# The output norm of an encoder layer: squares summed in the feature layout instead of on turned tokens, the gain applied before the turn, evictions by halves

## Chip, cores, metric

One core of a Trainium2 chip runs the whole program. The metric is device time of one execution in microseconds (us). Engines: TensorE (PE, with weight loads shown as PEld), VectorE (DVE), ScalarE (ACT), GpSimd (POOL), SyncE (SP, which here only issues DMAs).

## The reference, cut to what matters

One layer of a streaming encoder over 512 prompt tokens and 64 sample tokens with 1024 features. The last two steps are the down projection with its residual add, and a final RMSNorm with the gain `g_final`:

```
x = x + (silu(conv(a)) * b) @ w_down
...
def rmsnorm(x, g):
    x32 = x.astype(float32)
    y = x32 * rsqrt(mean(x32 * x32, axis=-1, keepdims=True) + EPS)
    return y * g
y_prompt = rmsnorm(xp, g_final)     # (1, 512, 1024)
y_sample = rmsnorm(xs, g_final)     # (1,  64, 1024)
```

## The kernel before

Every engine has its own instruction list, written out by hand; the lists meet at semaphores that count finished steps (`wait_ge`). The residual stream `x_t` lies in feature layout: 128 features on the partitions, `KT` = 8 feature tiles of `T` = 576 tokens (512 prompt, 64 sample) along the row. The outputs are wanted in token layout.

**The last down projection.** The hidden features are worked off in four chunks (`CHUNKS`). After the last chunk's up projection come 16 slots of down products, named by (e, q): e = 0 to 3 is the pair of output tiles 2e and 2e+1, q the factor of the weight block. A slot is 18 matmuls of 128x288 (`down_product`, L2742). Six slot buffers form a ring: ACT rounds a slot's weights to the high part (`slot_hi`, in its list six slots ahead, after the product that freed the buffer), DVE subtracts to get the low part (`slot_lo`). When a tile's products are done, DVE adds the accumulator to `x_t` (L2216) and counts `down_taken`. Tiles 0 and 1 come out of slots (0,2) and (0,3), and from then on tile 2e out of (e,1) and tile 2e+1 out of (e,3); tile 7 is the last. A product that starts a new accumulation waits until the tile before the last one has been taken.

**The output norm.** When the last tile is added, PE turns the five token tiles (four of 128 rows, one of 64) from `x_t` into the four PSUM tensors, eight 128x128 transposes for each (L2803; `final_bank(t)` is `ps[(t+2)%4]`). For every token tile ACT squares the 128x1024 PSUM tile with a running sum per row (L1555) and takes the root (L1558); DVE takes the reciprocal (L2234) and multiplies PSUM tile, reciprocal and a copy of `g_final` on all partitions into `y_tok` (L2235); SP stores the tile (L850, 512 KB, the last 256 KB). The fifth tile is turned when the first has left PSUM. `g_final` is fetched by POOL during the last chunk, spread over all partitions.

**The start.** POOL fetches rows of small parameters (`rows_in`), PE turns them into columns and DVE copies them into `gains`, one column for each 128 features (`NG` = 36).

Of the kernel before, what the change touches and what calls it, by code (L numbers as in the profile page):

```python
# [20 lines left out]
ACT = mybir.ActivationFunctionType  # L21
# [3 lines left out]
P = 128  # L25
# [16 lines left out]
def build(nc, a, o):  # L42

    TP, D = a["x_prompt"].shape[1:]
    TS = a["x_sample"].shape[1]
    T = TP + TS
    H = T // 2
    KT = D // P
# [18 lines left out]
    CHUNKS = [(0, 4), (4, 6), (10, 6), (16, 6)]  # L67
# [6 lines left out]
    DOWN_PAIRS = KT // 2  # L74
# [12 lines left out]
    for s in range(N_ENTRIES + LAG + 1):  # L87
        j, e = divmod(s, ENTRIES)
# [24 lines left out]
    with ctx:  # L113

        slab_bytes = (nc.sbuf_bytes_remaining - 96) // 32 * 32
        slab_at = (nc.sbuf_base + 31) // 32 * 32
        ctx.enter_context(nc.sbuf_tensor("slab", [P, slab_bytes // 4], F32))
        at = {}
        here = [0]

        def place(name, shape, dtype=F32):
            size = 4
            for s in shape[1:]:
                size *= s
# [13 lines left out]
        ident = place("ident", [P, P])  # L138
        causal = place("causal", [P, P])
        causal_s = place("causal_s", [P, DH])  # L140
        mean_w = place("mean_w", [P, P])
        eps = place("eps", [P, 1])
        one = place("one", [P, 1])
        NG = 4 * KT + GROUPS
        gains = place("gains", [P, NG])
        g_mix, g_xq, g_mkv, g_ffn = (gains[:, KT * k:KT * k + KT] for k in range(4))
        pool_scale = gains[:, 4 * KT:NG]
        conv_par = place("conv_par", [P, 4, NF])
        conv_hist = place("conv_hist", [P, 2, NF])
        b_f = place("b_f", [HEADS, 1])  # L150
# [172 lines left out]

        here[0] = at["b_hi"]
        y_tok = place("y_tok", [P, NT + 1, D])
        y_junk = place("y_junk", [P, D])
        g_final = place("g_final", [P, D])

        ps = [ctx.enter_context(nc.psum_tensor(f"ps{n}", [P, 2, 512], F32)) for n in range(4)]
        ACC, SC, OB = ps[0:2], ps[2], ps[3]  # L330
# [2 lines left out]
        def sem(name):  # L333
            return ctx.enter_context(nc.semaphore(name))
# [69 lines left out]
        y_turned, y_root, y_ready = sem("y_turned"), sem("y_root"), sem("y_ready")  # L404
        g_final_landed = sem("g_final_landed")
# [281 lines left out]
        def sums_of(n):  # L687

            return (sum_c, sum_d) if n == 1 else (sum_a, sum_b)

        def final_bank(t):
            return ps[(t + 2) % 4]

# [72 lines left out]
        def _(sp):  # L766
# [78 lines left out]
                raw_tile(r)  # L845

            for t in range(NT + 1):
                sp.wait_ge(y_ready, t + 1)
                y = o["y_prompt"][0, t * P:t * P + P, :] if t < NT else o["y_sample"][0]
                sp.dma_start(y, y_tok[0:y.shape[0], t, :]).then_inc(y_stored, 16)  # L850
            sp.wait_ge(y_stored, 16 * (NT + 1))
# [7 lines left out]
        def _(pool):  # L859
# [19 lines left out]
            pool.dma_start(rows_in[n:NG, 0, :], a["pool_scale"][0].rearrange("(k p) -> k p", p=P)).then_inc(rows_landed, 16)  # L879
            nc.gpsimd.memset(one[:], 1.0).then_inc(consts_ready, 1)  # L880
            nc.gpsimd.memset(mean_w[:], 1.0 / D).then_inc(consts_ready, 1)
            for x in flat_a + flat_b:
# [174 lines left out]
                    pool.wait_ge(conv_ready, 2 * f + 2)  # L1057
                    nc.gpsimd.tensor_copy(gate[:, GAP:GAP + 2], conv_hist[:, :, f + 1]).then_inc(edges_copied, 1)

            pool.wait_ge(slot_used, len(SLOTS) - 4 * DOWN_PAIRS)  # L1060
            pool.dma_start(g_final[:], a["g_final"].rearrange("(x d) -> x d", x=1).partition_broadcast(P)).then_inc(g_final_landed, 16)
            pool.wait_ge(conv_tok_ready, 1)
            pool.dma_start(o["conv_state_prompt"][0, 0].rearrange("s (f p) -> (s f) p", p=P), conv_tok[0:2 * NF, :]).then_inc(stored, 16)
            pool.dma_start(o["conv_state_sample"][0, 0].rearrange("s (f p) -> (s f) p", p=P), conv_tok[2 * NF:4 * NF, :]).then_inc(stored, 16)
# [3 lines left out]
        def _(act):  # L1068
# [6 lines left out]
            def copy(out, x, scale=1.0):  # L1075
                return nc.scalar.activation(out, x, ACT.Copy, scale=scale)  # L1076
# [447 lines left out]
            for g, (kind, k, e, q, _, _) in enumerate(SLOTS):  # L1524
                f0, nf = CHUNKS[k]
                f = f0 + e
                if kind == "up" and q < 3:
                    snapshot(k, e, g, q)
                slot_high(g + AHEAD)
                if kind == "up":  # L1530
                    if q == 0 and e > 0:
                        silu_of(f - 1)
                    if q == 2 and e > 0:
                        hidden_high(f - 1, e - 1)
                    if q == 5:
# [10 lines left out]
                if kind == "down" and f0 + nf == NF and (e, q) == (2, 0):  # L1546
                    act.wait_ge(y_turned, 1)
                    copy(conv_tok[:], ps[2][0:4 * NF, 0, 0:P]).then_inc(conv_tok_ready, 1)


            nc.scalar.activation(stat[:, 62:63], stat[:, 61:62], ACT.Sqrt)
            for t in range(NT + 1):
                r = P if t < NT else TS
                act.wait_ge(y_turned, t + 2)
                nc.scalar.activation(y_junk[0:r, :].rearrange("p (b c) -> p b c", b=2), final_bank(t)[0:r], ACT.Square,  # L1555
                                     accum_out=stat[0:r, 40 + t:41 + t]).then_inc(y_root, 1)
                act.wait_ge(y_root, 2 * t + 1)
                nc.scalar.activation(stat[0:r, 48 + t:49 + t], stat[0:r, 40 + t:41 + t], ACT.Sqrt, bias=eps[0:r],  # L1558
                                     scale=1.0 / D).then_inc(y_root, 1)


        @block.vector
        def _(dve):
# [3 lines left out]
            def after(ins):  # L1567
                link.inc(ins)
                dve.wait_ge(dve_link, link.now)
# [601 lines left out]
            for g, (kind, k, e, q, _, _) in enumerate(SLOTS):  # L2171
# [34 lines left out]
                    slot_sum(g + AHEAD + 1)  # L2206
                else:
                    slot_sum(g + AHEAD + 1)
                    if (e, q) == (0, 0) and k >= 1:
                        dve.wait_ge(hidden_ready, f0 + nf)  # L2210
                        low_hidden(f0 + nf - 1, nf - 1)
# [15 lines left out]
                        if what == "mixed low":  # L2227
                            mixed_low_of(m)

            dve.wait_ge(g_final_landed, 16)  # L2230
            for t in range(NT + 1):
                r = P if t < NT else TS
                dve.wait_ge(y_root, 2 * t + 2)
                after(nc.vector.reciprocal(stat[0:r, 56 + t:57 + t], stat[0:r, 48 + t:49 + t]))  # L2234
                nc.vector.scalar_tensor_tensor(y_tok[0:r, t, :].rearrange("p (b c) -> p b c", b=2), final_bank(t)[0:r],  # L2235
                                               stat[0:r, 56 + t:57 + t], g_final[0:r, :].rearrange("p (b c) -> p b c", b=2),
                                               mult, mult).then_inc(y_ready, 1)


        @block.tensor  # L2240
        def _(pe):
# [53 lines left out]
            for k in range(KT):  # L2295
                values(k)
                if k == 1:
                    pe.wait_ge(rows_landed, 16 * 4)
                    pe.wait_ge(more_rows_landed, 16 * 4)
                    pe.wait_ge(cols_ready, 1)  # L2300
                    turn(bank[:, 0:NG], rows_in[0:NG, 0, :], ident[0:NG, 0:NG])
                    turn(bank[:, 64:64 + 4 * NF], rows_in[0:4 * NF, 1, :], ident[0:4 * NF, 0:4 * NF])
                    turn(bank[:, 192:192 + 2 * NF], rows_in[0:2 * NF, 2, :], ident[0:2 * NF, 0:2 * NF])
                    for g in range(GROUPS):
                        ins = turn(bank[:, 256 + 16 * g:256 + 16 * g + NHIST], hist_tok[0:NHIST, g * P:g * P + P],
                                   ident[0:NHIST, 0:NHIST])
                    ins.then_inc(cols_turned, 1)
                if k == 2:
                    pe.wait_ge(x_scale, 1)
                    pe.wait_ge(cols_ready, 4)  # L2310
                    scale_turn(0, NT, P)
                if k + 2 < KT:
                    h_turn(k + 2)
                if k == 2:
                    pe.wait_ge(scale_rows, 1)
                    scale_turn(NT, NT + 1, TS)
# [472 lines left out]
                    else:  # L2789
                        down_product(g, k, range(half))  # L2790

            tiles = KT * len(CHUNKS)
            pe.wait_ge(down_taken, tiles - 2)
            pe.wait_ge(conv_tok_ready, 1)
            for t in range(NT + 1):
                r = P if t < NT else TS
                if t == NT:
                    pe.wait_ge(y_ready, 1)
                for k in range(KT):
                    if t == 0 and k == KT - 2:  # L2800

                        pe.wait_ge(down_taken, tiles)
                    ins = turn(final_bank(t)[0:r, k // 4, k % 4 * P:k % 4 * P + P], x_t[:, k, t * P:t * P + r], ident[:])  # L2803
                ins.then_inc(y_turned, 1)


_INS = ['x_prompt', 'x_sample', 'cache_fox_k', 'cache_fox_v', 'cache_fox_logf', 'state_pool', 'state_ffn_conv',
# [34 lines left out]
```

## Time and profile before

| | us |
|---|---|
| median of 3 runs | 863.5 (863.03 to 863.79) |
| profiled execution | 863.93 |
| its span, first to last instruction | 862.1 |
| PE busy in the span | 828.7 (96%) |
| DVE busy | 605.0 (70%) |
| ACT busy | 437.3 (51%) |
| POOL busy | 142.8 (17%) |

Matmuls are pipelined and their recorded durations overlap, so the busy time of PE is an upper view of its load. Idle time of an engine that is not the bottleneck costs nothing; what counts is which wait ends last. The last matmul of the last down product ends at 848.93 in the span, so the output norm and its stores are the remaining 13.2.

### The profile page before, as it was taken

What the parts mean: (1) busy time and instruction counts of PE and PEld (TensorE: products, weight loads), DVE (VectorE), ACT (ScalarE), POOL (GpSimd) and SP (SyncE); (2) the same over time, 40 slices, a digit from 0 to 9 for tenths busy, and PEclk for the clock granted to TensorE, in tenths of its full rate; (3) what the DMA queues carried; (4) which work ended last, traced back from release to release, by engine and by line L of the source; (5) the groups of instructions that cost most, each with busy time, mean ns of one, the idle gap of its engine ahead of it and who ended that gap; (6) DMA issues with size and microseconds to landing.
All of it is one profiled execution on the core that took longest, in us unless ns stands there. A gap on an engine that the chain in (4) does not pass through costs nothing.

```text
span 862.1 us, 15501 instructions
## 1 busy us (share of the span) xinstructions
PE 828.7 (96%) x5939; PEld 795.3 (92%) x5939; DVE 605.0 (70%) x1118; ACT 437.3 (51%) x793; POOL 142.8 (17%) x246
## 2 busy tenths in 40 slices
PE   5999999999999999999999999999999999999996
PEld 4798988988997899989998989999999999999995
DVE  3787766677665566554767898998469984699733
ACT  5677666646435554333334444665236652366523
POOL 5015566463000002000000100110001100011100
PEclk9999999999999999999999999999999999999999
DMA  6166434226327533120321323333233323332303
GB/s 215 49 223 169 135 94 113 81 74 233 95 73 284 204 98 122 51 73 2 97 74 50 97 74 100 97 100 110 86 89 89 90 89 95 90 98 86 115 24 111
DMA packets 105141, 91.57 MB, mean 106 GB/s; under 512 B 3008, under 2 KB 96406, under 8 KB 104819
## 3 DMA queue, kind: packets, MB, share of 16 engines
q1 hardware_dynamic: 99939, 73.51, 28.1%
q0 software_dynamic: 5136, 17.17, 6.6%
q8 instruction: 43, 0.70, 0.3%
q14 instruction: 23, 0.19, 0.1%
HBM read 81.32 MB, written 9.35 MB: 105 GB/s over the span
## 4 chain that ended last, share of the span: by engine, by line
PE 80%; DVE 11%; ACT 4%; issue 2%; DMA 2%; SPq 0%; DVEq 0%; ACTq 0%
PE ps L2731 23%; PE ps L434 19%; PE ps L2742 15%; PE ps L2381 4%; PE ps L2274 3%; PE ps L2561 3%; PE ps L2617 2%; PE ps L2567 1%; PE ps L2646 1%; PE ps L2667 1%; DVE w_lo L460 1%; PE ps L2361 1%; DMA x_tok<-in_x_sample 1%; DMA w_raw<-in_w_mk 1%; ACT w_hi L455 1%
## 5 line engine op out<-in xcount | busy, mean ns | idle before, releaser
L2731 PE MATMUL ps<-up_lo,slot_hi 128*128 128x288 f32 x504 | 149.2, 296 | 0.0
L2731 PE MATMUL ps<-up_hi,slot_lo 128*128 128x288 f32 x504 | 148.6, 295 | 0.0
L2731 PE MATMUL ps<-up_hi,slot_hi 128*128 128x288 f32 x504 | 148.5, 295 | 0.0
L1076 ACT ACTIVATE slot_hi<-raw 128x512 fp32r<-128x512 f32 (+2 forms) x118 | 64.6, 554 | 79.9 <-PE ps L2742 55.6
L2731 PEld LDWEIGHTS ps<-up_hi,slot_lo 128*128 128x128 f32 x504 | 95.1, 189 | 0.0
L2731 PEld LDWEIGHTS ps<-up_hi,slot_hi 128*128 128x128 f32 x504 | 95.0, 188 | 0.0
L2731 PEld LDWEIGHTS ps<-up_lo,slot_hi 128*128 128x128 f32 x504 | 94.8, 188 | 0.0
L464 DVE TENSOR_TENSOR slot_lo<-raw,slot_hi 128x512 fp32r<-128x512 f32 (+2 forms) x118 | 70.2, 598 | 31.5 <-ACT slot_hi L1076 31.0
L2742 PE MATMUL ps<-part_hi,slot_hi 128*128 128x288 f32 x352 | 75.5, 295 | 1.9 <-DVE x_t L2216 1.5
L2742 PE MATMUL ps<-part_lo,slot_hi 128*128 128x288 f32 x352 | 75.1, 295 | 0.0
L2742 PE MATMUL ps<-part_hi,slot_lo 128*128 128x288 f32 x352 | 75.0, 294 | 0.0
L1054 POOL COPY a_last<-gate 128x2 f32<-128x2 f32 x44 | 28.1, 668 | 274.3 <-DVE gate L2198 246.3
L434 PE MATMUL ps<-a_hi,w_hi 128*128 128x288 f32 x320 | 69.7, 300 | 2.9 <-DVE w_lo L460 0.9
L460 DVE TENSOR_TENSOR w_lo<-w_raw,w_hi 128x1024 fp32r<-128x1024 f32 x42 | 51.5, 1227 | 24.4 <-ACT w_hi L455 23.8
L434 PE MATMUL ps<-a_lo,w_hi 128*128 128x288 f32 x320 | 68.4, 296 | 0.0
L434 PE MATMUL ps<-a_hi,w_lo 128*128 128x288 f32 x320 | 68.4, 295 | 0.0
L455 ACT ACTIVATE w_hi<-w_raw 128x1024 fp32r<-128x1024 f32 x49 | 51.6, 1053 | 24.1 <-PE ps L434 15.4
L1076 ACT ACTIVATE slot_hi<-row_sum 128x512 fp32r<-128x512 f32 x72 | 45.4, 631 | 36.2 <-PE ps L2731 17.3
L2742 PEld LDWEIGHTS ps<-part_hi,slot_hi 128*128 128x128 f32 x352 | 56.3, 188 | 2.6 <-DVE x_t L2216 2.0
L2742 PEld LDWEIGHTS ps<-part_hi,slot_lo 128*128 128x128 f32 x352 | 56.5, 188 | 0.0
L2742 PEld LDWEIGHTS ps<-part_lo,slot_hi 128*128 128x128 f32 x352 | 56.4, 188 | 0.0
L434 PEld LDWEIGHTS ps<-a_hi,w_hi 128*128 128x128 f32 x320 | 51.4, 189 | 4.5 <-issue 2.5
(408 smaller groups left out, 2078.5 us busy)
## 6 DMA issues: line engine op xcount, KB each, us to landing
raw<-in_w_up SPq DMA_DIRECT2D x36, 512.0 KB, 4.9
raw<-in_w_down SPq DMA_DIRECT2D x12, 768.0 KB, 4.4
w_raw<-in_w_in SPq DMA_DIRECT2D x15, 512.0 KB, 4.1
w_raw<-in_w_o SPq DMA_DIRECT2D x8, 512.0 KB, 4.0
w_raw<-in_w_mq SPq DMA_DIRECT2D x8, 512.0 KB, 4.1
w_raw<-in_w_mo SPq DMA_DIRECT2D x8, 512.0 KB, 4.0
w_raw<-in_w_up SPq DMA_DIRECT2D x8, 512.0 KB, 3.8
w_raw<-in_w_mk SPq DMA_DIRECT2D x6, 512.0 KB, 3.9
```

The source lines that it names most:

```text
L434: mm = nc.tensor.matmul(acc[:, h, 0:H], w[slot][:, c], x[:, k, h * H:h * H + H], start=(k == first and w is w_hi and x is x_hi), stop=(k = ...
L455: nc.scalar.activation(w_hi[slot][:], w_raw[slot][:], ACT.Copy).then_inc(weight_hi_ready, 1)
L460: nc.vector.tensor_tensor(w_lo[slot][:], w_raw[slot][:], w_hi[slot][:].bitcast(F32), ALU.subtract).then_inc(weight_lo_ready, 1)
L464: return nc.vector.tensor_tensor(out, x, hi, ALU.subtract)
L1054: ins = nc.gpsimd.tensor_copy(a_last[:, 2 * g:2 * g + 2, f], gate[:, c:c + 2])
L1076: return nc.scalar.activation(out, x, ACT.Copy, scale=scale)
L2274: ins = mm(b, flat_a[x][:, k * T + t * P:k * T + t * P + P], w[n % 2][:, c], start=(k == 0 and x == 0 and w is w_hi), stop=(k == KT - 1 an ...
L2381: ins = mm(ACC[0][:, half, 0:H], w[n % 2][:, k * P:k * P + P], x[:, k, half * H:half * H + H], start=(k == 0 and w is w_hi and x is a_hi), ...
L2561: ins = mm(banks[t][:, h], x[:, k, t * P:t * P + P], w_hi[slot][:, h * 512:h * 512 + 512], start=(k == 0 and x is mem_hi), stop=False)
L2617: ins = mm(out, flat_b[x][:, col:col + P], kk[:, int(s == SAMPLE), k, :], start=(f == 0 and x == 0 and kk is mk_hi), stop=(f == 1 and x == 1))
L2731: ins = mm(up_bank(k, e, b), w[g % AHEAD][:, m * P:m * P + P], y[:, m, x], start=(first and m == 0 and w is slot_hi and y is up_hi), stop= ...
L2742: ins = mm(acc[:, h, 0:H], w[g % AHEAD][:, m * P:m * P + P], y[:, 2 * m + l, h * H:h * H + H], start=(l == 0 and m == 0 and w is slot_hi a ...
```

## The change

`g_final` becomes eight more columns of `gains`: one more small fetch by POOL and a wait for five such fetches at the start, and no fetch of the spread copy later. During the last down products, ACT makes of each finished `x_t` tile a square (`y_squared`) and a copy multiplied by its gain column (`y_gained`), DVE sums the squares of tiles 0 to 6 in `y_total`. ACT's preparatory root (which loads its function table) moves to slot (1,0). After the last add, DVE squares tile 7 and ACT makes its gained copy. PE turns tiles 0 to 6 of the first three token tiles, then forms the mean squares as one column for each token tile: for each of the five, two products with one column of `mean_w` (which holds 1/1024), one of `y_total` and one of tile 7's squares. Then it turns tile 7 of these three, and the two other token tiles when PSUM is free. ACT takes two roots (four columns, and one for the sample), DVE one reciprocal for all. Each token tile leaves PSUM in halves: ACT multiplies features 0 to 511 by the reciprocal, DVE features 512 to 1023. SP waits for both halves.

```diff
-        NG = 4 * KT + GROUPS
+        NG = 5 * KT + GROUPS
-        pool_scale = gains[:, 4 * KT:NG]
+        pool_scale, g_final = gains[:, 4 * KT:4 * KT + GROUPS], gains[:, 4 * KT + GROUPS:NG]
...
-        y_junk = place("y_junk", [P, D])
-        g_final = place("g_final", [P, D])
+        here[0] = at["up_lo"]
+        y_gained = place("y_gained", [P, KT, T])
+        y_squares = place("y_squares", [P, 2, T])
+        y_total = place("y_total", [P, T])
...
+        def mean_column(t):
+            return ps[1][:, 0, t:t + 1]
+        def y_squared(m):
+            return y_total[:] if m == 0 else y_squares[:, m % 2, :]
+        def y_half(t, h):
+            return y_tok[0:token_rows(t), t, h * 4 * P:(h + 1) * 4 * P]
+        SQUARES_AT = {(1, 0): (0, 1), (1, 2): (2,), (2, 0): (3,), (2, 2): (4,), (3, 0): (5,), (3, 2): (6,)}
+        SUMS_AT = {(1, 1): 1, (1, 3): 2, (2, 1): 3, (2, 3): 4, (3, 1): 5, (3, 3): 6}
...  SP
-                sp.wait_ge(y_ready, t + 1)
+                sp.wait_ge(y_by_act, KT + 2 + t + 1)
+                sp.wait_ge(y_by_dve, 2 + t + 1)
...  POOL
+            pool.dma_start(rows_in[n + GROUPS:NG, 0, :], a["g_final"].rearrange("(k p) -> k p", p=P)).then_inc(rows_landed, 16)
...
-            pool.wait_ge(slot_used, len(SLOTS) - 4 * DOWN_PAIRS)
-            pool.dma_start(g_final[:], a["g_final"].rearrange("(x d) -> x d", x=1).partition_broadcast(P)).then_inc(g_final_landed, 16)
...  ACT, in the loop over slots, after slot_high(g + AHEAD)
+                if kind == "down" and f0 + nf == NF:
+                    if (e, q) == (1, 0):
+                        nc.scalar.activation(stat[:, 62:63], stat[:, 61:62], ACT.Sqrt)
+                    for m in SQUARES_AT.get((e, q), ()):
+                        act.wait_ge(down_taken, LAST_DOWN + m + 1)
+                        if m >= 3:
+                            act.wait_ge(sum_ready, SUMS + m - 2)
+                        nc.scalar.activation(y_squared(m), x_t[:, m, :], ACT.Square).then_inc(x_squared, 1)
+                        copy(y_gained[:, m, :], x_t[:, m, :], g_final[:, m:m + 1]).then_inc(y_by_act, 1)
...  ACT, after the loop
-            for t in range(NT + 1):    # 5 x: Square with row sum from PSUM, then Sqrt
...
+            act.wait_ge(down_taken, LAST_DOWN + KT)
+            copy(y_gained[:, KT - 1, :], x_t[:, KT - 1, :], g_final[:, KT - 1:KT]).then_inc(y_by_act, 1)
+            act.wait_ge(y_turned, 2)
+            nc.scalar.activation(stat[:, 48:48 + NT], ps[1][:, 0, 0:NT], ACT.Sqrt, bias=eps[:]).then_inc(y_by_act, 1)
+            nc.scalar.activation(stat[0:TS, 48 + NT:49 + NT], mean_column(NT)[0:TS], ACT.Sqrt,
+                                 bias=eps[0:TS]).then_inc(y_by_act, 1)
+            act.wait_ge(y_by_dve, 2)
             for t in range(NT + 1):
+                act.wait_ge(y_turned, t + 3)
+                copy(y_half(t, 0), final_bank(t)[0:r, 0], stat[0:r, 56 + t:57 + t]).then_inc(y_by_act, 1)
...  DVE, in the loop, after slot_low and before the tile's add
+                    if f0 + nf == NF and (e, q) in SUMS_AT:
+                        m = SUMS_AT[e, q]
+                        dve.wait_ge(x_squared, X_SQUARED + m + 1)
+                        if m > 1:
+                            dve.wait_ge(sum_ready, SUMS + m - 1)
+                        nc.vector.tensor_tensor(y_total[:], y_total[:], y_squared(m), add).then_inc(sum_ready, 1)
...  DVE, after the loop
-            for t in range(NT + 1):    # 5 x: reciprocal, then PSUM * reciprocal * g_final over 1024
...
+            nc.vector.tensor_tensor(y_squared(KT - 1), x_t[:, KT - 1, :], x_t[:, KT - 1, :], mult).then_inc(y_by_dve, 1)
+            dve.wait_ge(y_by_act, KT + 2)
+            nc.vector.reciprocal(stat[:, 56:57 + NT], stat[:, 48:49 + NT]).then_inc(y_by_dve, 1)
+            dve.wait_ge(y_by_dve, 2)
             for t in range(NT + 1):
+                dve.wait_ge(y_turned, t + 3)
+                nc.vector.tensor_scalar(y_half(t, 1), final_bank(t)[0:r, 1], stat[0:r, 56 + t:57 + t], None,
+                                        mult).then_inc(y_by_dve, 1)
...  PE, after the last down product
-            for t in range(NT + 1):    # 5 x 8 transposes of x_t; tile 4 after tile 0 has left PSUM
...
+            pe.wait_ge(y_by_act, KT - 1)
+            pe.wait_ge(conv_tok_ready, 1)
+            for t in range(3):
+                turn_gained(t, range(KT - 1))
+            pe.wait_ge(sum_ready, SUMS + KT - 2)
+            pe.wait_ge(y_by_dve, 1)
+            for t in range(NT + 1):
+                r = token_rows(t)
+                mm(mean_column(t)[0:r], y_total[:, t * P:t * P + r], mean_w[:, 0:1], start=True, stop=False)
+                ins = mm(mean_column(t)[0:r], y_squared(KT - 1)[:, t * P:t * P + r], mean_w[:, 0:1], start=False, stop=True)
+            ins.then_inc(y_turned, 1)
+            pe.wait_ge(y_by_act, KT)
+            for t in range(3):
+                turn_gained(t, (KT - 1,)).then_inc(y_turned, 1)
+            pe.wait_ge(y_by_act, KT + 2)
+            turn_gained(3, range(KT)).then_inc(y_turned, 1)
+            pe.wait_ge(y_by_act, KT + 3)
+            pe.wait_ge(y_by_dve, 3)
+            turn_gained(NT, range(KT)).then_inc(y_turned, 1)
```

## Rows read from the trace of the kernel before

**Rows 1.** Chain that ended last, from 848: start us, us, what.

```profile
848.96 0.77 DVE x_t L2216
...
849.77 0.45 PE ps L2803 x2
...
850.24 1.12 ACT y_junk L1555 x2
...
851.98 1.28 DVE y_tok L2235
...
857.53 1.28 DVE y_tok L2235
```

**Rows 2.** Timeline of SP's DMA issues at the end: start us, us, what.

```profile
853.29 4.50 SPq L850 DMA_DIRECT2D out_y_prompt<-y_tok  x4
858.83 0.52 SPq L850 DMA_DIRECT2D out_y_sample<-y_tok  x1
```

**Rows 3.** Engine load by stretch; the last columns are TensorE clock, DMA share, GB/s.

```profile
854.00:854.50 0.50, 0.38 (x4) 0.12 (x2) 0.50 (x1) 0.47 (x3) 0.00 (x0) 1.00 0.75 303
...
857.00:857.50 0.50, 0.00 (x0) 0.00 (x0) 0.49 (x2) 0.00 (x0) 0.00 (x0) 1.00 1.02 418
...
861.00:861.50 0.50, 0.00 (x0) 0.00 (x0) 0.00 (x0) 0.00 (x0) 0.00 (x0) 0.50 0.17 41
...
854.00:859.50 5.50, 0.38 (x4) 0.12 (x2) 4.70 (x7) 2.90 (x8) 0.00 (x0) 0.86 0.93 375
859.50:861.20 1.70, 0.00 (x0) 0.00 (x0) 0.00 (x0) 0.00 (x0) 0.00 (x0) 0.50 0.75 174
```

**Rows 4.** Timeline of PE after the last down product.

```profile
848.76 0.82 PE L2803 MATMUL ps<-ident,x_t 128*128 128x128 f32 x6
...
849.77 3.06 PE L2803 MATMUL ps<-ident,x_t 128*128 128x128 f32 x26 [0.19 <-DVE x_t L2216]
```

**Rows 5.** Timelines of weight loads elsewhere: whose matmuls are short, and of the older norms.

```profile
22.95 0.32 PEld L2305 LDWEIGHTS ps<-ident,hist_tok 15*128 15x128 f32 x4
...
275.07 0.90 PEld L2530 LDWEIGHTS ps<-square_sum,mean_w 128*128 128x128 f32 x4
...
398.56 0.19 PEld L2658 LDWEIGHTS ps<-spt,mv_lo 128*128 128x128 f32 x1
398.66 0.19 PEld L2659 LDWEIGHTS ps<-spt,mv_lo 128*128 128x128 f32 x1
```

**Rows 6.** Groups by line and shape: count, busy us, mean ns, idle before.

```profile
L1076 ACT ACTIVATE v_out<-ps,stat 128x512 f32<-128x512 f32 x4 | 2.8, 702 | 0.0
...
L1076 ACT ACTIVATE b_hi<-ps,gains 128x576 fp32r<-128x576 f32 x4 | 3.0, 739 | 0.2 <-PE ps L2474 0.2
...
L1558 ACT ACTIVATE stat<-stat,eps 128x1 f32<-128x1 f32 x4 | 1.2, 294 | 0.1
...
L1904 DVE TENSOR_TENSOR square_sum<-square_sum,squares 128x576 f32<-128x576 f32 x16 | 12.0, 752 | 0.0
...
L1620 DVE COPY inv_rms<-ps 128x512 f32<-128x512 f32 x1 | 0.7, 692 | 0.8 <-PE ps L2257 0.8
...
L1616 DVE RECIPROCAL stat<-stat 128x5 f32<-128x5 f32 x1 | 0.2, 193 | 0.0
```

**Rows 7.** Timeline of ACT and DVE in the last down products.

```profile
822.74 0.53 ACT L1076 ACTIVATE slot_hi<-raw 128x384 fp32r<-128x384 f32 x1 [1.97 <-PE ps L2742]
...
829.87 0.76 DVE L2216 TENSOR_TENSOR x_t<-x_t,ps 128x576 f32<-128x576 f32 x1 [1.20 <-PE ps L2742]
...
835.20 1.28 ACT L1551 ACT_TABLE_LOAD   x1
```

**Rows 8.** Timeline of the start: POOL and PEld; last row: a DMA issue, KB, us to landing.

```profile
8.96 0.94 POOL L867 DMA_DIRECT2D wf_raw<-in_w_in  x1 [2.59 <-DMA x_tok<-in_x_prompt]
...
22.36 0.13 PEld L2301 LDWEIGHTS ps<-ident,rows_in 36*128 36x128 f32 x1 [0.35 <-issue]
...
rows_in<-in_g_mkv POOLq DMA_DIRECT2D x1, 4.0 KB, 5.2
```

More of the change, by code:

```diff
@@ L325, in build @@
         y_tok = place("y_tok", [P, NT + 1, D])
-        y_junk = place("y_junk", [P, D])
-        g_final = place("g_final", [P, D])
+        assert here[0] <= at["whole"]
+        here[0] = at["up_lo"]
+        y_gained = place("y_gained", [P, KT, T])
+        y_squares = place("y_squares", [P, 2, T])
+        y_total = place("y_total", [P, T])
+        assert here[0] <= slab_bytes
         ps = [ctx.enter_context(nc.psum_tensor(f"ps{n}", [P, 2, 512], F32)) for n in range(4)]
@@ L403, in build @@
         conv_tok_ready = sem("conv_tok_ready")
-        y_turned, y_root, y_ready = sem("y_turned"), sem("y_root"), sem("y_ready")
-        g_final_landed = sem("g_final_landed")
+        y_turned, y_by_act, y_by_dve = sem("y_turned"), sem("y_by_act"), sem("y_by_dve")
         stored, y_stored, v_stored = sem("stored"), sem("y_stored"), sem("v_stored")
@@ L692, in final_bank, with token_rows @@
             return ps[(t + 2) % 4]
+        def mean_column(t):
+            return ps[1][:, 0, t:t + 1]
+        def token_rows(t):
+            return P if t < NT else TS
+        def y_squared(m):
+            return y_total[:] if m == 0 else y_squares[:, m % 2, :]
+        def y_half(t, h):
+            return y_tok[0:token_rows(t), t, h * 4 * P:(h + 1) * 4 * P]
+        LAST_DOWN = KT * (len(CHUNKS) - 1)
+        X_SQUARED, SUMS = NT + 1, 2 * (KT + 1)
+        SQUARES_AT = {(1, 0): (0, 1), (1, 2): (2,), (2, 0): (3,), (2, 2): (4,), (3, 0): (5,), (3, 2): (6,)}
+        SUMS_AT = {(1, 1): 1, (1, 3): 2, (2, 1): 3, (2, 3): 4, (3, 1): 5, (3, 3): 6}
         H00, H10, H11, T1, T2, T3, T4 = range(FACTORS)
@@ L878, in _ @@
                 n += KT
[L879 removed]
+            pool.dma_start(rows_in[n:n + GROUPS, 0, :], a["pool_scale"][0].rearrange("(k p) -> k p", p=P)).then_inc(rows_landed, 16)
+            pool.dma_start(rows_in[n + GROUPS:NG, 0, :], a["g_final"].rearrange("(k p) -> k p", p=P)).then_inc(rows_landed, 16)
             nc.gpsimd.memset(one[:], 1.0).then_inc(consts_ready, 1)
@@ L1545, in _ @@
                         whole_high(m)
[L1546 to L1551, printed above, removed]
-            for t in range(NT + 1):
[L1553 to L1559, printed above, removed]
+                if kind == "down" and f0 + nf == NF:
[7 more added lines that the diff above has]
+                        copy(y_gained[:, m, :], x_t[:, m, :], g_final[:, m:m + 1]).then_inc(y_by_act, 1)
+                    if (e, q) == (2, 0):
+                        act.wait_ge(y_turned, 1)
+                        copy(conv_tok[:], ps[2][0:4 * NF, 0, 0:P]).then_inc(conv_tok_ready, 1)
@@ L2228, in _ @@
                             mixed_low_of(m)
-            dve.wait_ge(g_final_landed, 16)
-            for t in range(NT + 1):
[L2232 to L2237, printed above, removed]
+            dve.wait_ge(down_taken, LAST_DOWN + KT)
+            dve.wait_ge(sum_ready, SUMS + KT - 3)
+            nc.vector.tensor_tensor(y_squared(KT - 1), x_t[:, KT - 1, :], x_t[:, KT - 1, :], mult).then_inc(y_by_dve, 1)
+            dve.wait_ge(y_by_act, KT + 2)
+            nc.vector.reciprocal(stat[:, 56:57 + NT], stat[:, 48:49 + NT]).then_inc(y_by_dve, 1)
+            dve.wait_ge(y_by_dve, 2)
+            for t in range(NT + 1):
+                r = token_rows(t)
+                dve.wait_ge(y_turned, t + 3)
+                nc.vector.tensor_scalar(y_half(t, 1), final_bank(t)[0:r, 1], stat[0:r, 56 + t:57 + t], None,
+                                        mult).then_inc(y_by_dve, 1)
         @block.tensor
@@ L2297, in _ @@
                 if k == 1:
-                    pe.wait_ge(rows_landed, 16 * 4)
+                    pe.wait_ge(rows_landed, 16 * 5)
                     pe.wait_ge(more_rows_landed, 16 * 4)
@@ L2790, in _, with turn_gained @@
                         down_product(g, k, range(half))
-            tiles = KT * len(CHUNKS)
-            pe.wait_ge(down_taken, tiles - 2)
+            def turn_gained(t, tiles):
+                r = token_rows(t)
+                for m in tiles:
+                    ins = turn(final_bank(t)[0:r, m // 4, m % 4 * P:m % 4 * P + P], y_gained[:, m, t * P:t * P + r], ident[:])
+                return ins
+            pe.wait_ge(y_by_act, KT - 1)
             pe.wait_ge(conv_tok_ready, 1)
+            for t in range(3):
+                turn_gained(t, range(KT - 1))
+            pe.wait_ge(sum_ready, SUMS + KT - 2)
+            pe.wait_ge(y_by_dve, 1)
             for t in range(NT + 1):
[L2796 to L2804, printed above, removed]
+                r = token_rows(t)
+                mm(mean_column(t)[0:r], y_total[:, t * P:t * P + r], mean_w[:, 0:1], start=True, stop=False)
[9 more added lines that the diff above has]
+            turn_gained(NT, range(KT)).then_inc(y_turned, 1)
 _INS = ['x_prompt', 'x_sample', 'cache_fox_k', 'cache_fox_v', 'cache_fox_logf', 'state_pool', 'state_ffn_conv',
```

## The prediction

> **What bounds the kernel now.** I read the page first: PE is busy 96% of the span, so up to the last down product only work on PE's path counts, and the change adds nothing there. What it rewrites is the end, so I read the chain of waits from 848 on [rows 1]. It leaves PE with the last add of DVE (848.96), passes two transposes, ACT's square over a whole token tile (850.24) and then stays on DVE: five multiplications of 1.28 us, from 851.98 to 858.81, each 1.39 after the one before. By that view DVE's evictions set the end, and halving them should pay. The issues of the stores follow them closely: the first at 853.29, the last at 858.83 [rows 2].
>
> The load by stretch tells what the chain can't [rows 3]. The DMA engines start moving shortly after 854.0 (0.75 of the first half microsecond), and from then to 859.5 they are busy 0.93 of the time at 375 GB/s, with 418 in a half microsecond where the share is 1.02. So the four prompt stores keep the DMA engines nearly full already: 5.50 x 0.93 = 5.12 us of full-share work, which for 4 x 512 KB = 2.10 MB is 410 GB/s. The sample's store has half the bytes but costs 1.70 x 0.75 = 1.28 us, at 174 GB/s; it reads 64 partitions where the others read 128. Together 6.40 us of stream that no eviction can shorten. It takes 7.1 now, from about 854.05 to about 861.15 (0.17 of the last half microsecond that moves anything [rows 3]); only 0.7 of that is gaps. The time from the first store's issue to the end is therefore nearly fixed, and the question is when the first tile is ready, not when the last is.
>
> **The change part by part.** Times below are on the clock of this span; 862.1 of span stand in a profiled execution of 863.93, which lies 0.4 above the median of 863.5. I add the difference to the median.
>
> *Start.* The fifth small fetch costs POOL one more issue. POOL then sits idle for 2.59 us until a prompt tile lands [rows 8], which hides it; without that cover it would be about 0.5. Such fetches land 5.2 us after their issue, and PE first wants them at 22.36 [rows 8], long after. Eight more columns to turn and copy: under 0.05. The removed spread copy of the gain was a 512 KB fetch that nobody on the path waited for. Zero for all this.
>
> *During the last down products.* ACT gains eight operations of 128x576 up to slot (2,2) and six later, at most 0.74 each [rows 6], DVE six sums of 0.75. ACT's slots are 2.4 apart with 0.53 of work [rows 7], so in steady state there is room. The tight place is slot (1,0): after 822.74 + 0.53 the table load of 1.28 (now at 835.20, in idle time [rows 7]), a short root, then square, gain, square: 823.3 + 1.3 + 0.2 + 3 x 0.74 = 827.0. DVE waits for that second square ahead of taking tile 2, so tile 2 is taken not at 825.9 but at 827.0 + 2 x 0.75 = 828.5. Behind it on DVE wait a low part for a slot that PE reaches only about five slots (12 us) later, and PE's start of tile 4, which comes when slot (1,3) ends, just ahead of DVE's add at 829.87 [rows 7]. So 1.3 us of slack: I take zero and keep it as a rival.
>
> *After the last product.* PE doesn't wait for the last add: it turns tiles 0 to 6 of three token tiles, 21 transposes. 26 took 3.06 [rows 4], 0.118 each, so 2.47 from 848.76 to 851.2. Under them lie the last add (to 849.7), DVE's square of tile 7 (0.75, to 850.5) and ACT's last gained copy (0.74); without that cover the square would cost 0.75.
>
> Then the mean columns, the new step on the path. An older norm shows what one f32 product is made of: two products, four weight loads [rows 5]. So ten products are 20 weight loads with one moving column each; 16 are of 128 columns and 4, the sample's, of 64. No row has this shape. From below: four loads with short matmuls took 0.32, 0.08 each, but they hold 15 rows [rows 5]; that gives 16 x 0.08 + 4 x 0.04 = 1.4. From above: loads that don't overlap at all, at the full 0.19 that a 128x128 load lasts [rows 5], 16 x 0.19 + 4 x 0.10 = 3.4. Between: 128x128 loads under short matmuls of 64 columns, started 0.10 to 0.11 apart [rows 5]: 16 x 0.11 + 4 x 0.055 = 2.0. I take the last, the nearest in shape. Means done at 853.2.
>
> The page TensorE: Matmul & The Clock Gate of the Trainium skill (LDWEIGHTS (loading the stationary operand)) says that a load lasts by its columns and not its rows, 128 / 1.2 = 107 ns. The 0.10 to 0.11 of the 128-row loads agrees, the 0.08 of the 15-row loads does not; by that rule the step is an estimated 1.9, by the rows 2.0.
>
> Next ACT's two roots, 0.29 each and overlapped in part: 0.5, to 853.7. DVE's reciprocal of five columns 0.19 [rows 6], with about 0.1 of hand-over on each side: 854.05. Then the first halves, both at once: ACT 0.70, DVE 0.69 [rows 6]. The first token tile is ready at 854.75 and its store is issued at 854.8, against 853.29 now [rows 2]: 1.5 later. The removed steps (one square of 1.0, its row sum, a root, one multiplication of 1.28) are cheaper on the way to the FIRST tile than 21 transposes plus means; they were dear only summed over five tiles.
>
> After that the new order is fast: a tile each 0.6 to 0.7, the last half done by about 857.6 instead of 858.81. PE's tiles 3 and 4 (0.95 each) are turned by about 855.9, before they are wanted. But the stores now queue: 0.75 from issue to first packet as now, then 6.40 without gaps: 854.8 + 0.75 + 6.4 = 861.95, against 861.15. Sum: later first store +1.5, gaps that vanish -0.7, so **+0.8**: 864.7 by the profiled execution, **864.3** by the median.
>
> What stands against earlier evictions as such is the page DMA: Bandwidth & Descriptors of the Trainium skill (Where 436 GB/s comes from): 16 ports bound all of a core's transfers at 435 GB/s, and HBM at some 358. The trace goes past the second (410 and 418 GB/s) and stays under the first. By 435 for all bytes, sample included, the stream would take an estimated 5.4 and the time would be 863.3; by the rows 6.4.
>
> **The rivals.**
>
> A (forecast): stream full, first store 1.5 late. 864.3.
>
> B: the mean loads run as fast as the 15-row ones, or faster still: 0.6 to 0.9 less. 863.5. For it: those rows; against: their shape.
>
> C: the mean loads don't overlap: 3.4 instead of 2.0, all of it ahead of the first store. 865.7. Another half microsecond of hand-overs among PE, ACT and DVE would have the same effect. This is the rival on the slower side: from means of about 2.9 on it is slower than can be told from no change.
>
> D: the stores don't set the end, the evictions do, as the chain of waits says. The last half ends at 857.6 at the latest, 856.9 if the hand-overs are free: 858.81 - 856.9 = 1.9 earlier, 861.6. For it: the chain; against: the DMA share of 0.93 to 1.02.
>
> E: DVE's wait for the second square reaches PE. It decides from 1.3 us more than I count on ACT at slot (1,0); each us beyond goes to the end in full, say 865.5. For it: the tight sum; against: I counted ACT's operations unoverlapped.
>
> **How the numbers follow.** For this kernel 0.2% is 1.7 us, about what a measurement can tell from no change. Chances: A 0.60, B 0.15, C 0.13, D 0.05, E 0.07. A and B lie within 0.2% of 863.5 (861.8 to 865.2) but for 0.02 of A's upper end; C and E are slower; D is faster. So faster 0.05, same 0.73, slower 0.22. The range: B's lower end (863.5 less 0.6, as the hand-overs are also guesses) to C's 865.7 and a little over: 862.8 to 865.9.
>
> **What would show each step.** In the changed kernel's profile: 21 transposes without a gap after the last product; 20 weight loads whose starts are 0.1 apart; first store issued near 854.8, the last by about 858; DMA share near 1.0 with no dip between the prompt stores, ending near 862; the add of tile 2 some 2.6 late and PE with no idle time at slot (2,0). The prediction is wrong if the first store comes before 853 or after 856.5, if the DMA engines move more than 418 GB/s, or if PE stops inside the last down products.

## The result and the profile after

| | before | after |
|---|---|---|
| median, us | 863.5 | 865.96 |
| lowest to highest of 11 runs | 863.03 to 864.58 | 865.3 to 866.82 |
| profiled execution | 863.93 | 866.28 |
| its span | 862.1 | 864.5 |

The ratio is 1.0028 [1.0019, 1.0036]: slower by 2.46 us, where 0.8 was forecast, and just above the upper end of the range (865.9). One execution of run 5 below took 4606 us and is left out of every number. The end itself went as forecast, and what was not forecast was lost ahead of it. First the end, in the timeline of all engines of the kernel after (start us, us, what), which answers to [rows 1, 2, 4].

```profile
850.42 2.45 PE L2840 MATMUL ps<-ident,y_gained 128*128 128x128 f32 x21
850.62 0.76 DVE L2258 TENSOR_TENSOR x_t<-x_t,ps 128x576 f32<-128x576 f32 x1 [2.51 <-PE ps L2787]
851.41 0.76 DVE L2274 TENSOR_TENSOR y_squares<-x_t 128x576 f32<-128x576 f32 x1
...
852.61 0.30 PEld L2851 LDWEIGHTS ps<-mean_w,y_total 128*128 128x128 f32 x2
...
852.83 0.30 PEld L2852 LDWEIGHTS ps<-mean_w,y_squares 128*128 128x128 f32 x2
...
854.92 0.26 ACT L1588 ACTIVATE stat<-ps,eps 128x4 f32<-128x4 f32 x1 [2.72 <-PE ps L2852]
855.08 0.24 ACT L1589 ACTIVATE stat<-ps,eps 64x1 f32<-64x1 f32 x1
855.36 0.19 DVE L2276 RECIPROCAL stat<-stat 128x5 f32<-128x5 f32 x1 [3.19 <-ACT stat L1589]
...
855.58 2.97 ACT L1102 ACTIVATE y_tok<-ps,stat 128x512 f32<-128x512 f32 x5 [0.26 <-DVE stat L2276]
855.58 3.38 DVE L2281 TENSOR_SCALAR y_tok<-ps,stat 128x512 f32<-128x512 f32 x5
856.41 2.90 SPq L877 DMA_DIRECT2D out_y_prompt<-y_tok  x4
...
859.40 1.18 SPq L877 DMA_DIRECT2D out_y_sample<-y_tok  x1
```

From the last add to the first store's issue it is 856.41 - 850.62 = 5.79 us; before it was 853.29 - 848.96 = 4.33 [rows 1, 2]. That is the 1.5 of the forecast (1.46). From there to the end of the span it is 8.09, against 8.81: the forecast's -0.7 (-0.72). So the tail from the last add on went from 13.14 to 13.88, +0.74 for a forecast of +0.8. The load by stretch shows why the second term is no larger (the last columns are clock, DMA share, GB/s; compare [rows 3]).

```profile
857.00:857.50 0.50, 0.50 (x5) 0.25 (x3) 0.50 (x1) 0.50 (x2) 0.00 (x0) 1.00 0.53 213
857.50:858.00 0.50, 0.02 (x1) 0.00 (x0) 0.50 (x2) 0.50 (x2) 0.00 (x0) 1.00 1.01 401
858.00:858.50 0.50, 0.00 (x0) 0.00 (x0) 0.50 (x2) 0.50 (x2) 0.00 (x0) 1.00 1.02 418
...
860.50:861.00 0.50, 0.00 (x0) 0.00 (x0) 0.00 (x0) 0.00 (x0) 0.00 (x0) 1.00 1.07 426
...
863.00:863.50 0.50, 0.00 (x0) 0.00 (x0) 0.00 (x0) 0.00 (x0) 0.00 (x0) 0.50 1.00 221
863.50:864.00 0.50, 0.00 (x0) 0.00 (x0) 0.00 (x0) 0.00 (x0) 0.00 (x0) 0.50 0.02 0
```

From 857.5 on the DMA share stays near 1, at 393 to 426 GB/s and for the sample's rest at 221; no gap is left. The last store is issued at 859.40 and the bytes go on moving until 863.5.

What was not forecast shows in a plainer place: the last add itself is late, 850.62 against 848.96, and that is 1.66 of the 2.4 us by which the two profiled spans differ. DVE's adds to `x_t` mark the progress of PE through the whole kernel, with the same work between them in both. First the kernel before (timeline of DVE; last add of the first chunk, first add of the last chunk; the last add is in [rows 1]), then the kernel after.

```profile
534.60 0.75 DVE L2216 TENSOR_TENSOR x_t<-x_t,ps 128x576 f32<-128x576 f32 x1
...
817.85 0.76 DVE L2216 TENSOR_TENSOR x_t<-x_t,ps 128x576 f32<-128x576 f32 x1 [1.27 <-PE ps L2742]
```

The same adds after, with tile 2's beside them:

```profile
535.31 0.74 DVE L2258 TENSOR_TENSOR x_t<-x_t,ps 128x576 f32<-128x576 f32 x1
...
819.34 0.76 DVE L2258 TENSOR_TENSOR x_t<-x_t,ps 128x576 f32<-128x576 f32 x1 [1.28 <-PE ps L2787]
...
828.82 0.75 DVE L2258 TENSOR_TENSOR x_t<-x_t,ps 128x576 f32<-128x576 f32 x1
831.45 0.76 DVE L2258 TENSOR_TENSOR x_t<-x_t,ps 128x576 f32<-128x576 f32 x1 [0.28 <-PE ps L2787]
```

Of the 1.66, 0.71 are there at the last add of the first chunk (535.31 against 534.60). 0.95 come between it and the last add of all: 315.31 us against 314.36, in chunks of which two run before a single instruction of the new norm. In the last chunk, from its first add to its last, it is 31.28 against 31.11. PE has no gap there that could explain it; the load by stretch shows it busy all the time in both, first before, then after.

```profile
819.00:847.00 28.00, 28.00 (x214) 27.99 (x213) 8.15 (x14) 5.33 (x10) 1.08 (x2) 1.00 0.06 19
```

```profile
819.00:847.00 28.00, 28.00 (x213) 27.99 (x212) 12.82 (x20) 13.77 (x24) 1.09 (x2) 1.00 0.10 31
```

### The profile page after: what moved, and what is told of

Its sections match the earlier page's. It is cut to its first block, busy times and chain, and to the rows that moved or that the text cites. A ratio compares the mean times of both kernels' runs of the same rounds, so it can differ in the third digit from the quotient of the medians.

```text
span 864.5 us, 15569 instructions
## 1 busy us (share of the span) xinstructions
PE 832.4 (96%) x5959; PEld 798.8 (92%) x5959; DVE 606.5 (70%) x1121; ACT 443.8 (51%) x800; POOL 138.6 (16%) x246
## 4 chain that ended last, share of the span: by engine, by line
PE 81%; DVE 9%; ACT 4%; issue 2%; DMA 2%; SPq 0%; DVEq 0%; ACTq 0%
PE ps L2776 23%; PE ps L437 19%; PE ps L2787 16%; PE ps L2426 4%; PE ps L2319 3%; PE ps L2606 3%; PE ps L2662 2%; PE ps L2612 1%; PE ps L2691 1%; PE ps L2712 1%; PE ps L2406 1%; DVE w_lo L463 1%; DMA x_tok<-in_x_sample 1%; DMA w_raw<-in_w_mk 1%; PE ps L2480 1%
## 5 line engine op out<-in xcount | busy, mean ns | idle before, releaser
L1082 POOL COPY a_last<-gate 128x2 f32<-128x2 f32 x44 | 24.1, 578 | 275.1 <-DVE gate L2234 247.0
```

Of the source, the lines that this page charges most:

```text
L1082: ins = nc.gpsimd.tensor_copy(a_last[:, 2 * g:2 * g + 2, f], gate[:, c:c + 2])
```

## The experiments

**The theory** drawn from these two profiles: the tail costs what was forecast, and the rest is the place of the operands. The kernel puts its tiles one behind the other in SBUF, each rounded up to 32 bytes. Eight more columns make `gains` 192 bytes instead of 160, so all that lies behind it in the common order moves by 32 bytes: `x_t`, `part_hi` and `part_lo`, `up_lo`, two of the six slots. **The rivals**: ACT's and DVE's new work in the last down products slows PE there (the prediction's E, or contention), or the longer start does.

All times below are medians in us, with the ratio to the kernel before on the same chip and its 95% interval. The ratio isn't the quotient of the two medians; the two differ by up to 0.0008 (run 4), so differences of a few tenths of a microsecond between medians carry nothing.

**1. The kernel before, moved by 32 bytes.** Nothing else is changed.

```diff
-        gains = place("gains", [P, NG])
+        gains = place("gains", [P, NG + 8])
```

> The kernel before, with eight unused columns behind the gains and nothing else: every tile placed behind them moves up by 32 bytes, as it does in the changed kernel. Place theory (the matmuls that read the moved tiles run slower, which is the 1.7 us that the changed kernel is late before its output norm begins): 865.2, ratio 1.0019 to 863.5, and the last add of x_t comes some 1.5 later than at 848.96. Rival (the 1.7 comes from the change's own work, the fifth fetch, the wait for it, or squares and sums beside the last products): 863.5, ratio 1.000.

Measured: 865.33 against 863.15, 1.0026 [1.0016, 1.0035]. Its adds (timeline of DVE):

```profile
534.97 0.74 DVE L2216 TENSOR_TENSOR x_t<-x_t,ps 128x576 f32<-128x576 f32 x1
...
819.11 0.75 DVE L2216 TENSOR_TENSOR x_t<-x_t,ps 128x576 f32<-128x576 f32 x1 [1.28 <-PE ps L2742]
...
850.39 0.75 DVE L2216 TENSOR_TENSOR x_t<-x_t,ps 128x576 f32<-128x576 f32 x1 [4.02 <-PE ps L2742]
```

315.42 between the chunks' last adds and 31.28 in the last chunk: what the kernel after has (315.31 and 31.28), with the instructions of the kernel before. The tail is 863.6 - 850.39 = 13.21, that of before.

**2 and 3. Both kernels moved to 64 bytes.** In the kernel before:

```diff
-        gains = place("gains", [P, NG])
+        gains = place("gains", [P, NG + 16])
```

In the kernel after, whose `NG` is 8 larger:

```diff
-        gains = place("gains", [P, NG])
+        gains = place("gains", [P, NG + 8])
```

> The kernel before, with sixteen unused columns behind the gains: the same tiles move up by 64 bytes. If the remainder by 64 bytes is what counts, 863.5, ratio 1.000; if any move costs, or distances to other tiles count, it is slower, near 865; if larger multiples (the tiles now begin at multiples of 256) make it faster, it is below 863.

> The changed kernel with eight unused columns more, so that the tiles behind the gains stand 64 bytes and not 32 from where they stood before. Place theory: 1.7 of the 2.5 us vanish and only the later first store is left, 864.3, ratio 1.0009. Rival (the change's own work): 866.0, ratio 1.0028.

Measured: before 864.61, 1.0015 [1.0006, 1.0024]; after 864.62, 1.0011 [1.0002, 1.0020]. Sixty-four bytes cost the kernel before time too (315.15 and 31.27 in its trace), so the idea that only the remainder by 64 counts fell. Run 3 came out near the number expected of the place theory (1.0009), but by luck: its stretches of 315.14 and 31.26 did not go back to those of before. The two medians also say that the new norm costs nothing at this place; the traces say 0.62 more tail (13.84 against 13.22), which is less than the intervals can tell.

**4. The new norm with two token tiles first.** On the kernel of run 3: DVE squares tile 7 in two parts, PE forms the means of the first two token tiles ahead of the others, ACT and DVE take a root and a reciprocal for these two, so that their halves leave early.

```diff
-                ins = mm(mean_column(t)[0:r], y_squared(KT - 1)[:, t * P:t * P + r], mean_w[:, 0:1], start=False, stop=True)
-            ins.then_inc(y_turned, 1)
+            mean_of(range(2))
             pe.wait_ge(y_by_act, KT)
...
+            pe.wait_ge(y_by_dve, 2)
+            mean_of(range(2, NT + 1))
+            turn_gained(2, range(KT)).then_inc(y_turned, 1)
```

> The changed kernel with the tiles moved by 64 bytes as in the run before, and the tail in another order: DVE squares tile 7 for the first two token tiles first; PE turns tiles 0 to 6 of these two only, forms their two means, turns their tile 7 and goes on to the other three tiles; roots and reciprocals in two groups. If the time of the first store and 6.4 us of full stream set the end, the first store goes out near 852.8 on the clock of the kernel before instead of 854.8, and the time is 862.3, ratio 0.9986. If the last eviction sets the end, there is no gain against the run before: 864.3, ratio 1.0009.

Measured: 863.26, 1.0009 [0.9997, 1.0020], with executions from 861.98 to 866.88. That is the ratio expected if the evictions set the end. Its first store is issued at 852.70, 3.75 after the last add, where run 3 has 5.79. Of these 2.04 the tail got back 1.49 (12.35 for 13.84), and the trace shows what came between (load by stretch):

```profile
853.00:853.50 0.50, 0.50 (x6) 0.50 (x5) 0.33 (x2) 0.42 (x3) 0.00 (x0) 0.81 0.00 0
853.50:854.00 0.50, 0.50 (x4) 0.50 (x3) 0.13 (x1) 0.00 (x0) 0.00 (x0) 0.50 0.95 385
...
858.50:859.00 0.50, 0.00 (x0) 0.00 (x0) 0.00 (x0) 0.00 (x0) 0.00 (x0) 1.00 0.45 180
```

The granted clock fell to 0.50, the level of 1.2 GHz, soon after the products of one column. In the timeline of PE the transposes behind them are slow, and in SP's the sample's store is late, so that the DMA engines ran dry at 858.5:

```profile
852.65 4.51 PE L2859 MATMUL ps<-ident,y_gained 128*128 128x128 f32 x24
```

```profile
858.02 0.53 SPq L878 DMA_DIRECT2D out_y_sample<-y_tok  x1
```

24 transposes took 4.51 here, where the kernel after takes 2.45 for 21. So in this profile the last eviction does set the end, behind transposes that ran at the lower clock. The record has for each execution the granted clock averaged over the span: four of the twelve, with 0.999 or 1.000, took 861.98 to 862.93; the eight others, this profile among them, have 0.994 to 0.998 and took 863.08 to 866.88.

**5. The kernel after, at the places of before.** `eps`, `one` and `gains` share one tile of the bytes that they had before the change (224). The work is that of the kernel after, and all other tiles that both kernels have lie where they lay before.

```diff
-        eps = place("eps", [P, 1])
-        one = place("one", [P, 1])
...
-        gains = place("gains", [P, NG])
+        pack = place("pack", [P, 56])
+        gains, eps, one = pack[:, 0:NG], pack[:, NG:NG + 1], pack[:, NG + 1:NG + 2]
```

> The changed kernel with its eight new columns, and the two one-column constants eps and one, in a single tile that takes just the bytes which eps, one and the gains took before: every other tile stands where it stood in the kernel before. Place theory: the stretch from the last add of the first chunk to the last add of the fourth takes 314.4 us as in the kernel before (315.3 in the changed kernel, 315.1 in the kernels moved by 64 bytes), and only the tail's 0.7 is left: ratio 1.0009, some 864.2 against 863.5. Rival (the change's own work before the tail costs it): 315.3 and ratio 1.0028.

Measured: 863.8 against 863.14, 1.0007 [0.9998, 1.0016]. Timeline of DVE:

```profile
535.09 0.74 DVE L2257 TENSOR_TENSOR x_t<-x_t,ps 128x576 f32<-128x576 f32 x1
...
818.01 0.76 DVE L2257 TENSOR_TENSOR x_t<-x_t,ps 128x576 f32<-128x576 f32 x1 [1.27 <-PE ps L2786]
...
849.12 0.76 DVE L2257 TENSOR_TENSOR x_t<-x_t,ps 128x576 f32<-128x576 f32 x1 [2.52 <-PE ps L2786]
```

314.03 and 31.11: the figures of before are back, with all of the new squares, gains and sums in place. The tail is 863.0 - 849.12 = 13.88, that of after.

**6. The same with half of the stores' bytes.** The kernel leaves out features 512 to 1023 of every stored token.

```diff
-                sp.dma_start(y, y_tok[0:y.shape[0], t, :]).then_inc(y_stored, 16)
+                sp.dma_start(y[:, 0:D // 2], y_tok[0:y.shape[0], t, 0:D // 2]).then_inc(y_stored, 16)
```

> The changed kernel with tiles placed as before; of each token tile only features 0 to 511 are stored (the other half of y is left out), all else is done. Stream theory: 3.2 us of the 6.4 go, then the last eviction and a store's fixed time decide: 861.5 to 862, some 2.5 under the kernel with full stores. Eviction theory (the stores hide behind the evictions): no more than 0.5 less, 863.7.

Measured: 861.23, 0.9977 [0.9965, 0.9988], against 1.0007 of run 5. In its trace the last add comes at 847.28, and SP issues:

```profile
853.07 2.31 SPq L876 DMA_DIRECT2D out_y_prompt<-y_tok  x4
856.47 0.52 SPq L876 DMA_DIRECT2D out_y_sample<-y_tok  x1
```

The first store is 5.79 after the last add, to the hundredth what it is in the kernel after; every eviction is still there; the tail falls from 13.88 to 11.92. So the bytes set the end, as the forecast had it, not the evictions. It fell by 2.0 and not by 3.2, the half of 6.4, because the last store, issued at 856.47, now waits for its eviction, which came late while the clock was at 0.50 here too (19 transposes in 4.14 us): by the forecast's stream, as an estimate, the DMA engines would have been done with all bytes by 853.07 + 0.75 + 3.2 = 857.0.

**7. The kernel before with `part_hi`, `part_lo` and `up_lo` moved alone**, the first two by 32 bytes and the third by 64; `x_t` and the slots stay.

```diff
+        here[0] += 32
         part_hi = place("part_hi", [P, 6, T], F32R)
         part_lo = place("part_lo", [P, 6, T], F32R)
+        here[0] += 32
         up_lo = place("up_lo", [P, 4, FACTORS, H], F32R)
```

> The kernel before with 32 empty bytes before part_hi and 32 more before up_lo, so that only part_hi and part_lo (the moving operands of the down products) move by 32 bytes and up_lo by 64. Place theory: the last chunk's down products, from their first to their last add, take 31.3 as in the changed kernel and not 31.1, though ACT, DVE and POOL do just what they did; up products change only by up_lo. Rival (work on ACT and DVE beside the products slows PE): 31.1.

One execution: 863.62, which by itself says nothing at this size. Timeline of DVE:

```profile
533.64 0.75 DVE L2218 TENSOR_TENSOR x_t<-x_t,ps 128x576 f32<-128x576 f32 x1
...
817.36 0.75 DVE L2218 TENSOR_TENSOR x_t<-x_t,ps 128x576 f32<-128x576 f32 x1 [1.28 <-PE ps L2744]
...
848.65 0.75 DVE L2218 TENSOR_TENSOR x_t<-x_t,ps 128x576 f32<-128x576 f32 x1 [4.04 <-PE ps L2744]
```

315.01 and 31.29. In the last chunk the down products read `part_hi`, `part_lo` and the slots, and of these only the parts moved: that alone gives the whole 0.18 of that stretch. The down products of the two chunks before it show the same: 31.18 and 31.17 here, 30.98 and 30.97 in the kernel before, 31.19 and 31.18 in the kernel after.

**8. Two tiles first, at the places of before.** Run 4's order on run 5's places, and the third token tile is turned ahead of the last three means.

```diff
             turn_gained(1, (KT - 1,)).then_inc(y_turned, 1)
+            turn_gained(2, range(KT)).then_inc(y_turned, 1)
             pe.wait_ge(y_by_dve, 2)
             mean_of(range(2, NT + 1))
-            turn_gained(2, range(KT)).then_inc(y_turned, 1)
```

> The order that serves two token tiles first, with the tiles placed as in the kernel before, and with the third token tile turned before the last three means (in the run before, TensorE's granted clock was at half after these means, and the sample's store was issued only at 858.0). Stream theory: first store at 852.7 on the clock of the kernel before, full stream of 6.4, span 861.0, ratio 0.9985 to 0.9990. Eviction theory: the last eviction decides, and with it ending no earlier than 857.9, ratio 0.9995.

Measured: 862.52 against 863.14, 0.9991 [0.9982, 1.0000]: the only version with all its outputs below the kernel before, by 0.6 us, and the interval just reaches no change. It lies between what was expected of the stream (0.9985 to 0.9990) and of the evictions (0.9995). Its stores in the timeline of SP, after a last add at 847.06:

```profile
850.80 3.69 SPq L877 DMA_DIRECT2D out_y_prompt<-y_tok  x4
855.02 0.53 SPq L877 DMA_DIRECT2D out_y_sample<-y_tok  x1
```

And its load by stretch shows no gap:

```profile
853.00:853.50 0.50, 0.50 (x7) 0.50 (x6) 0.31 (x2) 0.25 (x2) 0.00 (x0) 1.00 1.00 410
...
855.00:855.50 0.50, 0.00 (x0) 0.00 (x0) 0.00 (x0) 0.00 (x0) 0.00 (x0) 1.00 1.00 410
```

The tail is 11.84. In this profile the clock stayed at 1.00 until the bytes were out, but not every execution was like it. Five of the twelve, this one among them, have an average clock of 1.000 and took 860.67 to 861.76; the seven others have 0.996 or 0.997 and took 862.46 to 863.58, about what the kernel before takes. So the profile shows the better kind, and a tail shorter by 1.3 than that of before need not show in full in the median. Where the clock fell in the seven, and whether the new place of the third tile or something else keeps it up in the five, isn't shown.

**All of them by landmarks.** Worked out from the timelines of DVE, in us: the last add of the first chunk, from there to the last add of all, the last chunk from its first add to its last, and the tail from the last add to the span's end.

| kernel | operands moved by | first chunk's end | to the last add | last chunk | tail |
|---|---|---|---|---|---|
| before | 0 | 534.60 | 314.36 | 31.11 | 13.14 |
| run 5 | 0 | 535.09 | 314.03 | 31.11 | 13.88 |
| run 6 | 0 | 532.92 | 314.36 | 31.11 | 11.92 |
| run 8 | 0 | 532.90 | 314.16 | 31.11 | 11.84 |
| after | 32 | 535.31 | 315.31 | 31.28 | 13.88 |
| run 1 | 32 | 534.97 | 315.42 | 31.28 | 13.21 |
| run 2 | 64 | 533.63 | 315.15 | 31.27 | 13.22 |
| run 3 | 64 | 534.52 | 315.14 | 31.26 | 13.84 |
| run 4 | 64 | 533.85 | 315.10 | 31.27 | 12.35 |
| run 7 | 32, 64 | 533.64 | 315.01 | 31.29 | 13.15 |

The third and fourth columns fall into two groups by place alone, whichever norm runs; the tail goes by the norm alone, whatever the place. The first chunk's end varies by 2.2 us among the kernels of the old place (532.90 to 535.09), so a single profile says nothing of how much of the shift's cost arises there.

Split by chunk, the same adds say more about the 0.95 between before and after. The down products of the last three chunks account for 0.59 of it (30.98, 30.97, 31.11 before; 31.19, 31.18, 31.28 after). The three stretches between the chunks, which are up products for the most part, account for 0.36 (73.55, 73.83, 73.92 before; 73.65, 73.98, 74.03 after). With 64 bytes the last two of these stretches take 73.85 and 73.85 (run 2), hardly more or less than before, while the down products stay at 31.15 to 31.27.

## Why the prediction was right at the end and wrong in the sum

*After the last product* was right term by term. The 21 transposes took 2.45 for a forecast of 2.47, without a gap. The means took 2.0 by the chain of waits of the kernel after:

```profile
850.59 2.29 PE ps L2840 x21
852.88 0.12 PE ps L2851 x2
853.00 0.22 PE ps L2852 x2
...
854.77 0.13 PE ps L2852 x2
```

That is 852.88 to 854.90, and the loads come as the 128-row rows of [rows 5] had it: two of them each 0.22. The Trainium skill agrees here (TensorE: Matmul & The Clock Gate, LDWEIGHTS (loading the stationary operand)): by its formula a load of 128 columns lasts 107 ns, which is the 0.11 of one load. Roots, reciprocal and hand-overs took 0.67 (854.89 to 855.56) for 0.85, the first halves with the store's issue 0.85 (855.56 to 856.41) for 0.75. The stores then queued: from the first issue to the span's end 8.09, where the forecast's sum gives 8.1 (854.8 to 862.9). So rival A held for the end, and B and C, which differed from it in the means, did not. D did not: counted from the last add, the last store was issued 8.78 after it instead of 9.87, and the end came later all the same; run 6 shows it from the other side. On the clock of the kernel before, which is 1.66 earlier, the first store was issued at 854.75, the last at 857.74 and the bytes ended at 861.8, for 854.8, 858 and 862 expected. One sign named for being wrong did appear: the DMA engines moved 426 GB/s in one half microsecond, over the 418 set as the limit, though the stream as a whole took what the sum gave it.

*During the last down products* was right as well. Tile 2 was taken at 828.82, where run 1, the old norm at the same places, has 826.42; since the two kernels stand 0.23 apart at the chunk's first add, that is 2.2 late, for a forecast of 2.6. Tile 3 was again taken as in run 1 (831.45 against 831.21). The reason is the one given, ACT's list at slot (1,0) in the kernel after:

```profile
824.79 1.28 ACT L1574 ACT_TABLE_LOAD   x1
826.09 0.20 ACT L1574 ACTIVATE stat<-stat 128x1 f32<-128x1 f32 x1
826.20 0.67 ACT L1579 ACTIVATE y_total<-x_t 128x576 f32<-128x576 f32 x1
826.77 0.76 ACT L1102 ACTIVATE y_gained<-x_t,gains 128x576 f32<-128x576 f32 x1
827.44 0.67 ACT L1579 ACTIVATE y_squares<-x_t 128x576 f32<-128x576 f32 x1
```

The second square ends at 828.11, and DVE sums and then adds. PE did not feel it: the last chunk takes 31.28 in the kernel after and in run 1, and 31.11 in run 5 and before. Rival E's wait reached DVE and not PE.

**The step that failed is *Start*: "Zero for all this"**, and with it the opening sentence that, up to the last down product, "the change adds nothing there". The prediction priced the eight columns as work (a fetch, some columns to turn and to copy) and not as bytes that push other tiles. Moving them costs the kernel before 0.26% [0.16%, 0.35%] with no other edit (run 1), which is 2.2 us; putting them back takes the kernel after from 1.0028 to 1.0007 (run 5). The forecast by itself, 864.3 to 863.5, is a ratio of 1.0009. That kernel has the fifth fetch and the eight columns too, and the first product of its projections starts at 12.27, where the kernel before has 12.78: as work they show no cost. So of the 2.46, about 0.7 is the new tail and about 1.8 is the place. The 0.7 is read from traces (13.88 against 13.21 at 32 bytes, 13.84 against 13.22 at 64); the ratios, 1.0028 against 1.0026 and 1.0011 against 1.0015, have intervals too wide to show it. Of the 1.8, the traces show 0.95 behind the first chunk; the rest would have to lie in the first 535 us, and isn't shown there. The time lies beside rival C's 865.7, but not by C's mechanism. In the traces PE is where it is lost: the stretches lengthen that PE fills without a gap (28.00 of 28.00 us), and the durations of DVE's adds stay at 0.75. Run 7 shows it for `part_hi` and `part_lo` as the moving operand of the down products. What remains open is the rule: 32 and 64 bytes both cost, no shift made it faster, and whether it is the distance between two tiles that are in use at once, or the address of one, wasn't tried. How the loss is shared out over the first 535 us is open too.

## What to carry to other kernels

Before costing an edit at nothing, ask what it does to the addresses of everything placed behind it; where PE is busy all the time, a control that moves the tiles and changes no work costs one line, and without it a loss of 0.2% goes to the wrong cause. When transfers fill the end, shorten the way to the first transfer and not the time to the last: evictions whose last store could go 1.1 us sooner gave nothing, the first two token tiles served early gave 2 us of tail in the profile of run 8. Counting progress by an operation that every version shares, such as an add per output tile, separates "slower all along" from "slower at the end" in one table.

## What was not expected of the hardware

**Place and matmul rate.** A shift of 32 or 64 bytes in operands lengthens the same matmuls' stretch from 314.0 to 314.4 us to 315.0 to 315.4, in ten traces without an exception.

**The clock within the tail.** In the profiles of the kernel after and of runs 3 and 8 it stayed at 1.00 until PE was done. In those of runs 4, 5 and 6 it fell to 0.50 shortly after the one-column products, with PE busy on either side. For run 5, the load by stretch:

```profile
853.00:853.50 0.50, 0.50 (x7) 0.48 (x7) 0.00 (x0) 0.08 (x1) 0.00 (x0) 1.00 0.00 0
853.50:854.00 0.50, 0.50 (x4) 0.24 (x4) 0.14 (x1) 0.32 (x2) 0.00 (x0) 0.69 0.00 0
854.00:854.50 0.50, 0.50 (x3) 0.50 (x4) 0.47 (x2) 0.42 (x1) 0.00 (x0) 0.50 0.00 0
```

Its last 19 transposes took 4.08 instead of 2.70, and its tail is still 13.88: the stores hid it. In run 4, where the stores began 2 us sooner, it showed. What decides whether it falls isn't shown: the kernel after and run 5 have the same instructions there.

**A store from 64 partitions.** At a DMA share of 1.00 the sample's bytes move at 221 GB/s where the prompt's move at 401, as [rows 3] had hinted. The Trainium skill gives a reason (SBUF — State Buffer, Door 1: The DMA port swizzle (why `[64,N]` ≈ `[32,N]`)): partitions 0 to 63 reach half of the 16 ports. No run here moves the sample's rows to other partitions.
